# Two-layer hybrid model kernel: selected attention's index logits over 64 rows and its values into 64 columns, in pairs of heads

## What is computed

```
def block(args):                      # one block of 128 queries, 4 blocks
    rel = relu(einsum('bqhd,bsd->bqhs', qib, ki))        # 4 index heads of 64, one index key for all
    score = einsum('bqh,bqhs->bqs', wib, rel)            # weighted sum over the index heads
    score = where(causal, score, -inf)
    _, sel = top_k(score, 128)
    logits = einsum('bqhd,bqkd->bqhk', qb, k_sel) * 64 ** -0.5   # 8 heads of 64, one key for all
    p = softmax(where(valid, logits, -inf))
    return einsum('bqhk,bqkd->bqhd', p, v_sel)           # one value of 64 for all heads
```

## Time and profile before

| | us |
|---|---|
| three runs | 1351.18, 1351.52, 1353.28 |
| median | 1351.52 |
| the profiled execution | 1351.5 |
| its span, first to last instruction | 1349.6 |
| TensorE busy | 1321.1 |
| VectorE / ScalarE / GpSimd busy | 784.8 / 551.6 / 607.0 |
| granted TensorE clock, mean over the span | 0.994 |
| TensorE L2003, 24 records | 377, 486 or 592 ns each |
| TensorE L2033, 160 records | 275 ns each (median) |

### The profile page before, as it was taken

The page is one execution under the profiler, slowest core; times in us unless marked ns, Lnnn a source line. Parts: engine busy times, 40 slices in busy tenths (PEclk is TensorE's granted clock), DMA queues, the critical chain, the costliest instruction groups (busy, mean ns, idle before and its releaser), DMA issues.

```text
span 1349.6 us, 18163 instructions
## 1 busy us (share of the span) xinstructions
PE 1321.1 (98%) x6253; PEld 1065.7 (79%) x6253; DVE 784.8 (58%) x1093; ACT 551.6 (41%) x862; POOL 607.0 (45%) x293
## 2 busy tenths in 40 slices
PE   8999989999999999999999999999999999999997
PEld 7688867886778888888888777777788888888886
DVE  6798885633456777777633489886633333332322
ACT  6446786533243222233232335665532223223222
POOL 4598873432234444444444334232344444444431
PEclk9999999999999999999999999999999999999999
DMA  6123311221122222223222222111222222233231
GB/s 233 61 94 110 110 63 47 86 86 48 47 94 92 95 93 93 97 105 105 94 106 87 92 78 88 54 63 48 78 94 93 93 101 101 93 105 107 87 97 73
DMA packets 31877, 121.21 MB, mean 90 GB/s; under 512 B 3536, under 2 KB 3664, under 8 KB 31568
## 3 DMA queue, kind: packets, MB, share of 16 engines
q1 hardware_dynamic: 31536, 119.81, 26.2%
q10 hardware_dynamic: 288, 0.69, 0.2%
HBM read 118.40 MB, written 2.10 MB: 89 GB/s over the span
## 4 chain that ended last, share of the span: by engine, by line
PE 76%; issue 13%; POOL 5%; DVE 4%; ACT 2%; POOLq 0%; ACTq 0%; DVEq 0%
PE acc L1761 62%; POOL weights_low L639 4%; PE acc L1935 3%; PE aux L1870 2%; PE acc L2309 1%; PE aux L2184 1%; PE aux L2195 1%; PE aux L2210 1%; POOL conv L688 1%; PE acc L1829 1%; PE acc L1903 1%; PE aux L2033 1%; DVE a_low L1432 1%; DVE aux L1257 1%; ACT weights_high L714 1%
## 5 line engine op out<-in xcount | busy, mean ns | idle before, releaser
L639 POOL TENSOR_TENSOR weights_low<-weights_raw,weights_high 128x1024 fp32r<-128x1024 f32 (+1 forms) x204 | 527.9, 2588 | 709.3 <-ACT weights_high L714 708.5
L714 ACT CAST weights_high<-weights_raw 128x1024 fp32r<-128x1024 f32 (+1 forms) x202 | 222.0, 1099 | 497.3 <-PE acc L1761 460.6
L1761 PE MATMUL acc<-a_high,weights_high 128*128 128x512 f32 x944 | 375.9, 398 | 2.1 <-DVE a_low L1432 1.1
L1761 PE MATMUL acc<-a_high,weights_low 128*128 128x512 f32 x944 | 368.4, 390 | 0.0
L1761 PE MATMUL acc<-a_low,weights_high 128*128 128x512 f32 x944 | 368.2, 390 | 0.0
L1761 PEld LDWEIGHTS acc<-a_high,weights_high 128*128 128x128 f32 x944 | 177.8, 188 | 43.1 <-issue 3.3
L1761 PEld LDWEIGHTS acc<-a_low,weights_high 128*128 128x128 f32 x944 | 177.7, 188 | 37.6 <-issue 1.9
L1761 PEld LDWEIGHTS acc<-a_high,weights_low 128*128 128x128 f32 x944 | 177.6, 188 | 37.4
L1230 DVE TENSOR_TENSOR residual<-acc,residual 128x512 f32<-128x512 f32 (+1 forms) x63 | 43.3, 687 | 168.9 <-PE acc L1761 129.8
L1761 PE MATMUL acc<-h_high,weights_high 128*128 128x512 f32 x330 | 128.9, 391 | 0.0
L1761 PE MATMUL acc<-h_high,weights_low 128*128 128x512 f32 x330 | 128.4, 389 | 0.0
(11 more groups left out here) (396 smaller groups left out, 1939.6 us busy)
## 6 DMA issues: line engine op xcount, KB each, us to landing
weights_raw<-w SPq DMA_DIRECT2D x172, 512.0 KB, 3.2
weights_raw<-w SPq DMA_DIRECT2D x32, 704.0 KB, 4.0
residual<-xT SPq DMA_DIRECT2D x8, 256.0 KB, 6.7
out<-y_tok SPq DMA_DIRECT2D x4, 512.0 KB, 3.2
mem_raw<-memT SPq DMA_DIRECT2D x1, 1024.0 KB, 8.6
mem_tok<-mem SPq DMA_DIRECT2D x1, 1024.0 KB, 10.6
lru_weights<-blockdiag ACTq DMA_DIRECT2D x1, 512.0 KB, 3.4
sine<-positions SPq DMA_DIRECT2D x1, 256.0 KB, 7.4
```

The source lines that it names most:

```text
L639: g.tensor_tensor(weights_low[:, s, 0:cols], weights_raw[:, s, 0:cols], weights_high[:, s, 0:cols].bitcast(F32), ALU.subtract).then_inc(we ...
L714: a.copy(weights_high[:, s, 0:cols], weights_raw[:, s, 0:cols]).then_inc(weight_high, 1)
L1761: last = t_.matmul(acc[:, bank, 0:cols], w[:, s, wide], x_[:, k0 + k, 0:cols], start=start and k == opens and n == 0, stop=stop and k == c ...
```

## The change

The index key is kept once, roped like a query, the same 64 rows in both halves of the partitions. The logits of two index heads are issued together: each takes its 64 rows of `qiT` and of `kiT`, in two cuts of columns, the heads in turn. An item of odd number issues nothing; the pair waits for the score operations of both items whose banks it takes, and the pair of items 2 and 3 waits for the third rope. The values are kept once, 64 columns wide (`v_tok`). Values are issued at the odd head for both heads, in turn, each into its own 64 rows of `aux[4]`; nothing is issued at the even one. `probT` has four buffers, and ScalarE's wait moves accordingly. Memsets and the second value product go.

```
--- before.py
+++ after.py
@@ -157,8 +157,8 @@
         kv = sb("kv", [P, T], where=s1)
         kiwi = sb("kiwi", [P, T], where=s1)
         kT = sb("kT", [P, 2, T], where=s1)
-        kiT = sb("kiT", [P, 2, T], where=s1)
-        v_pad = sb("v_pad", [P, 2, QB, P], where=s1)
+        kiT = sb("kiT", [P, T], where=s1)
+        v_tok = sb("v_tok", [P, QB, HALF], where=s1)
         wi = sb("wi", [P, QB, IDX_HEADS], where=s1)
         token_tables = sb("token_tables", [P, 2, QB, 16], where=s1)
         cosine = sb("cosine", [P, T], where=s1)
@@ -177,7 +177,7 @@
         product = sb("product", [P, 2, T], where=s1b)
         masked = sb("masked", [P, 2, T], where=s1b)
         prob = sb("prob", [P, 3, T], where=s1b)
-        probT = sb("probT", [P, 2, T], where=s1b)
+        probT = sb("probT", [P, 4, T], where=s1b)
         att = sb("att", [P, T], where=s1b)
         att_inverse = sb("att_inverse", [P, T], where=s1b)
         wide_inverse = sb("wide_inverse", [P, T], where=s1b)
@@ -231,7 +231,7 @@
         acc = ctx.enter_context(nc.psum_tensor("acc", [P, 2, T], F32))
         aux = [ctx.enter_context(nc.psum_tensor(f"aux{i}", [P, T], F32)) for i in range(6)]
         angle = aux[4][:]
-        q_tok = [qiT[:, 0], qiT[:, 1], kiT[:, 0], kiT[:, 1]]
+        q_tok = [qiT[:, 0], qiT[:, 1], kiT[:], kiwi[:]]
         x_square = ([aux[5][:]] + [gate[:, k] for k in range(1, 4)] + [score[:, k] for k in range(3)]
                     + [product[:, 0]])
 
@@ -866,9 +866,9 @@
                 elif what == "prob":
                     w = w_of(j)
                     act.wait_ge(probT_done, j + 1)
-                    if j >= 2:
-                        act.wait_ge(heads_done, j - 1)
-                    a.copy(probT[:, j % 2, 0:w], turn_bank(what, j)[:, 0:w]).then_inc(probT_ready, 1)
+                    if j >= 4:
+                        act.wait_ge(heads_done, j - 3)
+                    a.copy(probT[:, j % 4, 0:w], turn_bank(what, j)[:, 0:w]).then_inc(probT_ready, 1)
                 elif what == "total":
                     act.wait_ge(inverse_ready, j + 1)
                     if j:
@@ -1159,10 +1159,7 @@
             own = Steps(dve, dve_steps)
 
             own.step(v.memset(glu[:, :, 0:TAPS - 1], 0.0))
-            own.step(v.memset(kiT[0:HALF, 1], 0.0))
             own.step(v.memset(kT[0:HALF, 1], 0.0))
-            own.step(v.memset(v_pad[:, 0, :, HALF:P], 0.0))
-            own.step(v.memset(v_pad[:, 1, :, 0:HALF], 0.0))
             own.settle()
             v.memset(least, 0.0).then_inc(glu_clear, 1)
 
@@ -1280,11 +1277,13 @@
                 elif what == "v":
                     dve.wait_ge(v_done, 1)
                     blocks = aux[5][:].rearrange("p (b f) -> p b f", f=P)
-                    for sub in range(2):
-                        v.tensor_tensor(v_pad[:, sub, :, sub * HALF:(sub + 1) * HALF], blocks[:, :, HALF:P],
-                                        by_token(tok_factor, HALF), ALU.mult).then_inc(v_out, 1)
+                    v.tensor_tensor(v_tok[:], blocks[:, :, HALF:P], by_token(tok_factor, HALF), ALU.mult
+                                    ).then_inc(v_out, 1)
                 elif what == "key":
-                    key_rope((kiT, kT)[j], aux[0][:], aux[1][:])
+                    if j:
+                        key_rope(kT, aux[0][:], aux[1][:])
+                    else:
+                        rope(kiT[:], aux[0][:], cosine[:], aux[1][:])
                 elif what == "query":
                     dve.wait_ge(table_copied, 1)
                     rope(qiT[:, j], qiT[:, j], aux[4][:], aux[2 + j][:])
@@ -1987,7 +1986,7 @@
                     pe.wait_ge(wi_out, 1)
                     blocks_of(kv, aux[5]).then_inc(v_done, 1)
                 elif what == "mem_spread":
-                    pe.wait_ge(v_out, 2)
+                    pe.wait_ge(v_out, 1)
                     pe.wait_ge(mem_factor, 1)
                     for b in range(MB):
                         last = t_.matmul(aux[5][:, b * P:(b + 1) * P],
@@ -1996,12 +1995,21 @@
                     last.then_inc(mem_spread, 1)
                 elif what == "index":
                     qb, h = INDEX[j]
-                    pe.wait_ge(roped, 3 if h >= 2 or j == 3 else 2)
+                    if j % 2:
+                        continue
+                    pe.wait_ge(roped, 3 if h >= 2 or j == 2 else 2)
                     if j >= 4:
-                        pe.wait_ge(rel_used, j - 3)
+                        pe.wait_ge(rel_used, j - 2)
                     w = (qb + 1) * P
-                    t_.matmul(aux[j % 4][:, 0:w], qiT[:, h // 2, qb * P:(qb + 1) * P], kiT[:, h % 2, 0:w],
-                              start=True, stop=True).then_inc(index_logits, 1)
+                    cut = w // 2
+                    for at in range(0, w, cut):
+                        for head in range(2):
+                            half = slice(head * HALF, (head + 1) * HALF)
+                            last = t_.matmul(aux[(j + head) % 4][:, at:at + cut],
+                                             qiT[half, h // 2, qb * P:(qb + 1) * P], kiT[half, at:at + cut],
+                                             start=at == 0, stop=at + cut == w)
+                            if at + cut == w:
+                                last.then_inc(index_logits, 1)
                 elif what == "fill":
                     memory(*n)
                 elif what == "logits":
@@ -2024,16 +2032,21 @@
                     last.then_inc(probT_done, 1)
                 elif what == "value":
                     qb, h = DSA[j]
+                    if h % 2 == 0:
+                        continue
                     pe.wait_ge(probT_ready, j + 1)
-                    if j == 0:
-                        pe.wait_ge(v_out, 2)
-                    if qb and h == 0:
+                    if j == 1:
+                        pe.wait_ge(v_out, 1)
+                    if qb and h == 1:
                         pe.wait_ge(att_scaled, qb)
                     for b in range(qb + 1):
-                        last = t_.matmul(aux[4][:, h // 2 * P:(h // 2 + 1) * P], v_pad[:, h % 2, b],
-                                         probT[:, j % 2, b * P:(b + 1) * P],
-                                         start=h % 2 == 0 and b == 0, stop=h % 2 == 1 and b == qb)
-                    last.then_inc(heads_done, 1)
+                        for head in range(2):
+                            half = slice(head * HALF, (head + 1) * HALF)
+                            last = t_.matmul(aux[4][half, h // 2 * P:(h // 2 + 1) * P], v_tok[:, b],
+                                             probT[:, (j - 1 + head) % 4, b * P:(b + 1) * P],
+                                             start=b == 0, stop=b == qb)
+                            if b == qb:
+                                last.then_inc(heads_done, 1)
                 elif what == "heads":
                     pe.wait_ge(inverse_wide, j + 1)
                     bank_free(what, j)
```

## The result

In 22 runs each the change took 1354.31 us (median; 1350.02 to 1357.81) and the kernel before 1351.02: a ratio of **1.0017, 95% interval 1.0009 to 1.0025** (by the medians alone it would be 1.0024, since the runs of the change lie mostly in two clusters, 1350 to 1352 and 1354 to 1358 us). The loss is small: it lies within the 0.2% that the prediction could not tell from no change, and to which it gave 0.56. The profiled execution of the change took 1353.0 us (span 1351.2).

The account below looks back on a forecast made before the run. TensorE was taken to lead in the index stage, 117 to 138 us and the tail, VectorE to pace most of 138 to 212. Terms -1.1 - 0.2 + 0.5 - 1.2 = -2.0 us gave 1349.5 us, range 1345.8 to 1352.6.

Parts of the forecast that it names:

- TensorE's own saving: On TensorE alone: index logits 7.7 to 5.1 us, values 17.8 to 13.9 us, together 6.5 us less.
- The rival without overlap: Half-array pairs do not overlap, so TensorE gets 6.2 us of switches and no relief: +4, 1355.5 us; chance 0.03.
- Index stage, -1.1: 44 to 58 us: paired index logits end the last score earlier, -1.1 us, bounds -0.4 and -2.2.
- 117 to 138, -0.2: Stretch where TensorE leads: step 0's value leaves the path, value groups grow; -0.2 us, bounds -0.4 and +0.3.
- 138 to 212, +0.5: Stretch VectorE mostly paces: pairs come later at the ends of blocks 0 and 1; +0.5 us, bounds -1.0 and +0.9.
- the clock: TensorE's granted clock: one low stretch of 3.4 us more or less is up to 1.7 us; in the range's low side only.
- Tail, -1.2: 212 to 222 us, TensorE without a pause: last four values as two pairs, 3.56 to 2.40 us; bounds -0.8 and -1.7.
- Rival C: 138 to 212 us: each pair holds up the next logits by 0.31 us; slower, 1352.7 to 1354.5 us; chance 0.10.
- Rival A: TensorE is the bound throughout, so all 6.5 us come through: 1345.0 us; chance 0.11.

Follow-up runs that it names:

- e4: The change plus 33 identity products that nothing reads, put into TensorE's gaps, against the kernel before: 1350.77 us, ratio 0.9994.
- e10: The kernel before with each head's value products moved behind the next logits, against the kernel before: 1350.71 us, ratio 1.0001.
- e7: The kernel before with two heads' value products issued together at the odd head, in full width over padded values: 1353.21 us, ratio 1.0024.
- e12: The change with three half rounds of memory products moved from 117 to 138 us into steps with idle time, against the kernel before: 1346.36 us, ratio 0.9964.

## Why the prediction was wrong

**TensorE's own saving: right, slightly small.** Halves overlap; the index groups hold it 5.0 us (5.1 forecast), a last pair 1.02 (1.20). The rival without overlap is out. The rule of the Trainium skill ("TensorEngine Tiling (Array Packing)", Theoretical Speedup), up to 2x at a dimension of 64, would give 0.89 for that pair; the trace gives 1.02, so a factor of 1.75.

**Index stage, -1.1: half.** -0.55 in the profiled change, -0.6 to the mean in the index part alone. I had let the last pair's score follow at 57.0; waits for banks of 0.39 and 0.17 us and ScalarE's 1.35 put it later. It lay within my bounds.

**117 to 138, -0.2: nothing.** The masks of the change stand 0.56 us earlier at 119 and 0.53 earlier at 140.

**138 to 212, +0.5: the sign was right, the size at its bound, and the sequel was missed.** The masks at the end of block 0 came 0.34 us later, as forecast. But the ends of blocks 1 and 2 cost some 0.3 and 0.2 more, so that at 208 the masks stand, with the 1.6 of the first low stretch taken off, 0.4 later than before: +0.9, my upper bound. Forecast was 2 us more of idle time; it was 4.7, as the pair waits for ScalarE's cast and copy, which I had not put in its way, and as the widened inverse comes later.

**The failed step is the clock.** I wrote that "one such stretch more or less is up to 1.7 us", as if chance alone placed them, and put it on the low side of the range alone. (One on the high side, 1351.5 + 1.7 = 1353.2 us, would not have reached 1354.31 either; there were two.) The size was right (some 1.6), the assumption wrong: the change adds idle time in the one stage that had some already, the mean clock falls from 0.9954 to 0.9927, and two more low stretches ahead of the mean turn about -1.1 into +2.1. In the sum the term stood at nothing; it measured some 3.2 us in the profiled execution. e4 supports this: the same half-array work with its gaps filled has no low stretch there and a mean clock of 0.9962. Where in a given execution a stretch falls is still partly chance. Without the clock the forecast would have missed as well, by 0.9 us at the mean, but inside its bounds.

**Tail, -1.2: about right.** With 1.6 us for the low stretch at 211.8 taken off, the mean's shift (2.1) less that of the mask near 203 (2.0) is 0.1 - 1.6 = -1.5.

**Rival C** had the side but not the mechanism. It charged each pair 0.31 us against waiting logits and gave 1352.7 to 1354.5, and the time fell into that span mostly by luck: VectorE's waits for logits in 138 to 212 rose from 1.6 to 2.4 us, short of the 3 that it asked for. What would have told more was the chain of ScalarE behind the odd head, and a look at what stood in TensorE's queue in its place. Rival A, all 6.5 us, didn't occur in any kernel, though 3.3 us of difference did with five half rounds moved.

Not tried: pairs issued so that ScalarE's cast stands behind the copy; how the low stretches after the mean (340, 767, 843) are placed, which differed between executions of one kernel.

## What to carry to other kernels

Work taken from TensorE in a stage that another engine paces becomes idle time, and in this stage more idle time, in gaps of 1 to 2 us, went with more stretches of low clock over the runs, so that less work took longer. Before making TensorE faster in such a stage, look for real work of a neighbouring full stretch that can be moved into the gaps, and do both together: the change alone cost 0.17%, the move alone gave 0.20%, and both 0.46%. And grouping two small steps into one has a price of its own: the single steps had been cover for someone's wait.

## What was not expected of the hardware

- The clock fell after several gaps of 1 to 2 us each; the longest in the profiled change was 2.18 us. The same gaps, 1.64 and 1.75 us, left it at 1.00 in another execution of the same kernel.
- 33 products that nothing reads brought 2.0 us in the change (1352.77 to 1350.77), some 1.3 us of their own time already paid; the kernel before stood at 1349.06 with nine of them and at 1350.50 without, which the ratio's interval doesn't tell from no change.
- A stretch of 3.4 us at a granted clock of 0.55 cost 1.57 us in the same kernel, inside a stage that VectorE paces for the most part.
- The same kernel's runs differ by up to 7.8 us (1350.02 to 1357.81), and in step with their mean clock, 0.996 to 0.990.
- Of two kernels with about as much idle time, one kept its clock (e10: 7.9 us, 0.9962) and one did not (e7: 8.3 us, 0.9938), and e12 lost it at 5.2. What in the pattern of the gaps decides stays open.
